# Down projection of a feed-forward block: column groups in pairs, two of eight tile pairs with seven block products

## What is computed

```python
hn = rms_norm(h, norm_ffn[i])
h = h + jnp.square(jax.nn.relu(hn @ ffn_w1[i])) @ ffn_w2[i]      # 256x2048 @ 2048x8192, then 256x8192 @ 8192x2048
gate = jax.nn.sigmoid(rms_norm(h, norm_ple[i]) @ ple_w_gate[i])
h = h + (p[i] @ ple_w_proj[i]) * gate
```

## Time and profile before

| | |
|---|---|
| median of 3 runs | 2211.09 us |
| span of the profiled execution | 2209.0 us |
| PE busy | 2197.2 us (99%) |
| DVE busy | 1445.2 us (65%) |
| ACT busy | 1106.9 us (50%) |
| POOL busy | 550.7 us (25%) |
| mean granted TensorE clock | 0.999 |

### The profile page before, as it was taken

One profiled execution on the slowest core, in us unless ns is written; L12 is line 12 of the kernel. 1 busy time (PEld: TensorE's weight loads), 2 busy tenths in 40 slices (PEclk: granted clock), 3 DMA queues, 4 the chain that ended last, 5 costly groups with the idle time before them and its releaser, 6 DMA issues.

```text
span 2209.0 us, 34195 instructions
## 1 busy us (share of the span) xinstructions
PE 2197.2 (99%) x11625; PEld 1878.9 (85%) x11625; DVE 1445.2 (65%) x1925; ACT 1106.9 (50%) x1654; POOL 550.7 (25%) x531
## 2 busy tenths in 40 slices
PE   9999999999999999999999999999999999999998
PEld 7888988888888888888888887888888888888887
DVE  6877765555664565555566667567785688756875
ACT  6445555453453454445455455565553455534553
POOL 3202220350240141053000033005540245403431
PEclk9999999999999999999999999999999999999999
DMA  7675335556555555556555653545555555555554
GB/s 254 232 230 163 115 128 204 170 190 208 191 190 192 189 189 192 186 192 193 187 185 179 227 171 135 193 160 188 195 188 196 192 183 192 189 195 192 186 209 149
DMA packets 118072, 414.21 MB, mean 188 GB/s; under 512 B 12896, under 2 KB 18048, under 8 KB 117472
## 3 DMA queue, kind: packets, MB, share of 16 engines
q1 hardware_dynamic: 111600, 401.37, 53.9%
q10 hardware_dynamic: 6384, 11.70, 1.7%
HBM read 409.29 MB, written 2.15 MB: 186 GB/s over the span
## 4 chain that ended last, share of the span: by engine, by line
PE 98%; DVE 1%; ACT 1%; issue 0%; DMA 0%; DVEq 0%; ACTq 0%
PE bank L486 33%; PE bank L494 17%; PE bank L543 7%; PE bank L545 7%; PE bank L544 7%; PE bank L1059 4%; PE bank L1060 4%; PE bank L1061 4%; PE bank L599 1%; PE bank L601 1%; PE bank L600 1%; PE bank L619 1%; PE bank L994 1%; PE bank L656 1%; PE bank L796 1%; PE bank L798 1%
## 5 line engine op out<-in xcount | busy, mean ns | idle before, releaser
L1100 DVE TENSOR_TENSOR wboth<-raw,wboth 128x1024 fp32r<-128x1024 f32 x756 | 982.2, 1302 | 607.8 <-ACT wboth L1802 607.1
L1802 ACT CAST wboth<-raw 128x1024 fp32r<-128x1024 f32 x756 | 790.9, 1049 | 711.5 <-PE bank L545 241.6
L486 PE MATMUL bank<-A,wboth 128*128 128x512 f32 x2928 | 705.1, 391 | 0.3 <-DVE wboth L1100 0.3
L486 PEld LDWEIGHTS bank<-A,wboth 128*128 128x128 f32 x2928 | 537.0, 188 | 104.6 <-issue 1.0
L494 PEld LDWEIGHTS bank<-A,wboth 128*128 128x128 f32 x2928 | 376.7, 191 | 14.8
L494 PE MATMUL bank<-A,wboth 128*128 128x256 f32 x2928 | 384.0, 283 | 0.0
L543 PE MATMUL bank<-wboth,H 128*128 128x512 f32 x576 | 224.6, 390 | 0.0
L545 PE MATMUL bank<-wboth,H 128*128 128x512 f32 x576 | 224.2, 389 | 0.0
L544 PE MATMUL bank<-wboth,H 128*128 128x512 f32 x576 | 224.1, 389 | 0.0
L2257 POOL TENSOR_TENSOR bias<-z,rs 128x256 f32<-128x256 f32 x64 | 75.7, 1182 | 481.2 <-DVE z L1131 391.6
L2257 POOL TENSOR_TENSOR PT<-z,rs 128x256 f32<-128x256 f32 x88 | 73.4, 835 | 465.4 <-DVE z L1131 464.8
(11 more groups left out here) (293 smaller groups left out, 2409.1 us busy)
## 6 DMA issues: line engine op xcount, KB each, us to landing
raw<-wstream SPq DMA_DIRECT2D x756, 512.0 KB, 3.3
bias<-bias_rows ACTq DMA_DIRECT2D x6, 512.0 KB, 5.4
x<-xrows ACTq DMA_DIRECT2D x1, 2048.0 KB, 10.0
bias<-grows ACTq DMA_DIRECT2D x2, 1024.0 KB, 6.1
out<-x SPq DMA_DIRECT2D x8, 256.0 KB, 2.1
x<-xT SPq DMA_DIRECT2D x7, 256.0 KB, 4.6
pA<-bias_rows ACTq DMA_DIRECT2D x2, 512.0 KB, 8.9
Sm<-grows ACTq DMA_DIRECT2D x1, 1024.0 KB, 5.8
```

The lines of the kernel that those rows point to most:

```text
L486: last = nc.tensor.matmul(bank(j)[:, :], whi[:, s, cols(i)], moving(j, k), start=(k == 0), stop=(k == K - 1))
L1100: V.tensor_tensor(wlo[:, s, :], raw[:, s, :], whi[:, s, :].bitcast(F32), ALU.subtract).then_inc(lo_ready, 1)
L1802: C.copy(whi[:, s, :], raw[:, s, :]).then_inc(hi_ready, 1)
```

## The change

In fd0, fd1 and fd2 two groups of 512 columns are taken together: a piece now holds one row of tiles (128 hidden values) by 1024 columns, and a column pair (`cp` 0 and 1) has 16 pieces. It accumulates into four banks, banks 0 to 3 for the first pair (`main_bank`), 4 to 7 for the second. Two of the eight pairs of pieces (`FAST` = 3 and 5: pieces 6 and 7, 10 and 11) see their product as one of 2 x 2 blocks (two halves of the tokens, two tiles of hidden values, two halves of the columns) and form it with seven block products of sums of blocks in place of eight. Four more banks (`side_bank`) hold the products that go into more than one block.

The sums are made so: POOL makes those of `H` in the up stage (`mix`, three operations behind the 8th and the 12th unit); ACT and POOL split them. DVE (`t_first`) and POOL (`t_rest`) make those of the weights, ACT (`t_highs`) and DVE (`t_lows`) split them. In the end DVE adds the side banks to `x` and to two scratch tiles (`sides_in`), POOL adds the scratch tiles (`corners`), and DVE adds the main banks (`mains_in`). The counters are old semaphores used again (`Again`). PE waits for four banks at the start of a column pair, and the projection's third group waits for `mains_in` of fd2. The loops over the two halves of a down stage are unrolled on PE, DVE and ACT, and POOL's loop over the units is unrolled too. fd3 stays as it was. The stream of the weights is laid out to suit, on the host.

```diff
+FAST = (3, 5)
+FAST_LAST = 13
+CARRY_IN = 16 + 1
...
-                    with pe.Fori(0, 2) as it:
-                        for f in range(2):
-                            down(it, f)
+                    for cp in range(2):
+                        down_pair(c, cp)
+
+            def product(bank, a_hi, a_lo, w_hi, w_lo, start=False, stop=False):
+
+                nc.tensor.matmul(bank[:, :], a_hi, w_hi, start=start, stop=False)
+                nc.tensor.matmul(bank[:, :], a_hi, w_lo, start=False, stop=False)
+                return nc.tensor.matmul(bank[:, :], a_lo, w_hi, start=False, stop=stop)
+
+            def down_pair(c, cp):
+
+                _, fd, o = chunk_at(c)
+                p = o * 64 + (PB[fd] + 16 * cp)
+                for j in range(4):
+                    pe.wait_ge(z_ready, o * 24 + (UB[fd] + (8 if cp else j + 1)))
+                for i in range(16):
...
+                    pe.wait_ge(lo_ready, p + (i + 1))
+                    if cp == 0:
+                        pe.wait_ge(ff_ready, c * CH + (i + 1))
...
+                    if not second:
...
+                        product(side_bank(cp, ONE), H[:, i, 0, 0:P], H[:, i, 1, 0:P], whi[:, s, half[0]], wlo[:, s, half[0]],
+                                lone, final).then_inc(piece_used, 1)
+                        continue
+                    product(main_bank(cp, 0), H[:, i, 0, 0:P], H[:, i, 1, 0:P], whi[:, s, half[0]], wlo[:, s, half[0]])
+                    product(main_bank(cp, 2), mixed[0][:, n, 3, :], mixed[1][:, n, 3, :], whi[:, s, half[1]], wlo[:, s, half[1]]).then_inc(piece_used, 1)
+                    t0 = c * 8 + (4 * cp + 2 * n)
+                    pe.wait_ge(*t_lo.at(t0 + 1))
+                    product(side_bank(cp, FIVE), mixed[0][:, n, 1, :], mixed[1][:, n, 1, :], Tcopy[0][:, 0, :], Tcopy[1][:, 0, :], lone, final)
+                    product(side_bank(cp, SEVEN), mixed[0][:, n, 0, :], mixed[1][:, n, 0, :], Tcopy[0][:, 1, :], Tcopy[1][:, 1, :], lone, final)
+                    pe.wait_ge(*t_lo.at(t0 + 2))
+                    product(side_bank(cp, SIX), mixed[0][:, n, 2, :], mixed[1][:, n, 2, :], Tcopy[0][:, 2, :], Tcopy[1][:, 2, :], lone, final)
+                    product(main_bank(cp, 1), H[:, i, 0, P:2 * P], H[:, i, 1, P:2 * P], Tcopy[0][:, 3, :], Tcopy[1][:, 3, :]).then_inc(t_used.sem, 1)
...
+                if f == 2:
+                    pe.wait_ge(*banks_taken.at(8 * (FF_CHUNKS - 1)))
...
+            def t_first(c, o, p0, q, n):
...
+                V.tensor_tensor(Tsum[:, 0, :], raw[:, x, 0:WIDE], raw[:, x, WIDE:], ALU.add).then_inc(t_sum.sem, 1)
+                dve.wait_ge(raw_landed[y], o * 256 + ((p0 + q + 1) // SLOTS + 1) * 16)
+                V.tensor_tensor(Tsum[:, 1, :], raw[:, x, WIDE:], raw[:, y, WIDE:], ALU.add).then_inc(t_sum.sem, 1)
+
+            def t_lows(c, i, n):
...
+                for h in range(2):
+                    dve.wait_ge(*t_hi.at(t0 + (h + 1)))
+                    V.tensor_tensor(Tcopy[1][:, 2 * h:2 * h + 2, :], Tsum[:, 2 * h:2 * h + 2, :], Tcopy[0][:, 2 * h:2 * h + 2, :].bitcast(F32),
+                                    ALU.subtract).then_inc(t_lo.sem, 1)
...
+            def sides_in(c, o, fd, cp):
+
+                dve.wait_ge(*t_used.at(c * 4 + (2 * cp + 2)))
...
+                V.tensor_copy(cross, one).then_inc(side_copied.sem, 1)
+                dve.wait_ge(*side_copied.at(c * 2 + (cp + 1)))
+                V.tensor_tensor(corner, six, cross, ALU.subtract).then_inc(z_ready, 1)
+                V.tensor_tensor(quarter(cp, 0, 0), quarter(cp, 0, 0), one, ALU.add).then_inc(z_ready, 1)
+                dve.wait_ge(z_ready, z0 + 1)
+                V.tensor_tensor(cross, corner, five, ALU.subtract).then_inc(z_ready, 1)
+                V.tensor_tensor(quarter(cp, 1, 0), quarter(cp, 1, 0), seven, ALU.add)
+                V.tensor_tensor(quarter(cp, 1, 1), quarter(cp, 1, 1), seven, ALU.subtract).then_inc(z_ready, 1)
+
+            def mains_in(c, o, fd, cp):
+
+                dve.wait_ge(piece_used, o * 64 + (PB[fd] + SLOTS + 16 * cp + 16))
+                dve.wait_ge(z_ready, o * 24 + (4 + UB[fd] + 4 * cp + 4))
+                dve.wait_ge(*corners_added.at(c * 6 + (3 * cp + 3)))
+                for j in range(4):
+                    dst = quarter(cp, j % 2, j // 2)
+                    V.tensor_tensor(dst, dst, main_bank(cp, j)[:, :], ALU.add).then_inc(banks_taken.sem, 1)
+
+            def down_pairs(c, fd, o):
+
+                p, p0 = o * 64 + PB[fd], PB[fd]
+                for q in range(LEAD, 32 + AHEAD):
...
+                    if before is not None and y:
+                        t_lows(c, q - 1, before)
+                    if second:
+                        dve.wait_ge(*t_more.at(c * 8 + (q // 16 * 4 + 2 * n + 2)))
+                    if AHEAD <= q:
+                        split_lo(p + q, (p0 + q) % SLOTS, WIDE if second == 0 else PW)
+                    if after is not None and not x:
+                        t_first(c, o, p0, q + 1, after)
+                    cp, i = divmod(q - LEAD, 16)
+                    if cp < 2 and i == FAST_LAST:
+                        sides_in(c, o, fd, cp)
+                    if (cp, i) in ((1, CARRY_IN - 16), (2, CARRY_IN - 16)):
+                        mains_in(c, o, fd, cp - 1)
...
+            def t_highs(c, i, n):
...
+                C.copy(Tcopy[0][:, 0:2, :], Tsum[:, 0:2, :]).then_inc(t_hi.sem, 1)
+                act.wait_ge(*t_more.at(s0 * 2 + 2))
+                C.copy(Tcopy[0][:, 2:4, :], Tsum[:, 2:4, :]).then_inc(t_hi.sem, 1)
...
+            def mix(c, n, a, b):
...
+                G.tensor_tensor(mixsum[:, n, 0:2, :], both, a[:, late].unsqueeze(1).to_broadcast([P, 2, P]), ALU.subtract).then_inc(mix_sum.sem, 1)
+                pool.wait_ge(*mix_sum.at(s0 + 1))
+                G.tensor_tensor(mixsum[:, n, 2, :], mixsum[:, n, 1, :], a[:, early], ALU.add).then_inc(mix_sum.sem, 1)
+                pool.wait_ge(*mix_sum.at(s0 + 2))
+                G.tensor_tensor(mixsum[:, n, 3, :], b[:, early], mixsum[:, n, 2, :], ALU.subtract).then_inc(mix_sum.sem, 1)
+
+            def t_rest(c, cp, i, n):
...
+                G.tensor_tensor(Tsum[:, 2, :], Tsum[:, 0, :], raw[:, y, WIDE:], ALU.add).then_inc(t_more.sem, 1)
+                pool.wait_ge(*t_more.at(t0 + 1))
+                G.tensor_tensor(Tsum[:, 3, :], Tsum[:, 2, :], raw[:, y, 0:WIDE], ALU.add).then_inc(t_more.sem, 1)
+
+            def corners(c, o, fd, cp):
+
+                pool.wait_ge(z_ready, o * 24 + (4 + UB[fd] + 4 * cp + 4))
+                for t, f, src, op in ((1, 0, corner, ALU.subtract), (0, 1, cross, ALU.add), (1, 1, cross, ALU.add)):
+                    dst = xN[:, t, (2 * cp + f) * WIDE:(2 * cp + f + 1) * WIDE]
+                    G.tensor_tensor(dst, dst, src, op).then_inc(corners_added.sem, 1)
...
-                with pool.Fori(0, 4) as it:
+                for it in range(4):
...
+                    if fast and 2 * it + 1 in FAST:
+                        mix(c, FAST.index(2 * it + 1), tB[:, 2, :], tB[:, 3, :])
+                if fast:
+                    down_pairs(c, fd, o)
```

More of the change, by code:

```diff
@@ L174, in cmp_due, with fast_piece @@
     return [g for g in range(KVG) if (8 * g + CMP_AT[step] if g < KVG - 1 else CMP_AT_LAST[step]) == i]
+FAST = (3, 5)
+FAST_LAST = 13
+CARRY_IN = 16 + 1
+def fast_piece(i):
+    m, second = divmod(i % 16, 2)
+    return (FAST.index(m), second) if m in FAST else (None, None)
 def turn_of(n):
@@ L191, in __call__, with __init__, at @@
         self.eng.wait_ge(self.sem, self.n)
+class Again:
+    def __init__(self, sem, reached):
+        self.sem, self.reached = sem, reached
+    def at(self, n):
+        return self.sem, n + self.reached
 def program(nc, xT, pT, wstream, consts, setup, params, grows, xrows, out):
@@ L220, in program @@
         pA = sb("pA", [P, 2, 2, S], FR)
+        with nc.sbuf_tensor("Tboth", [P, 2, 4, WIDE], FR) as Tboth:
+            pass
         y = sb("y", [P, DT, S])
@@ L250, in ring @@
             return flat[:, a:a + n * w].rearrange("p (n w) -> p n w", n=n)
+        Tsum = ptf.rearrange("p (n c) -> p n c", n=4)
+        Tcopy = [Tboth[:, h, :, :] for h in range(2)]
+        kTf = kT[:, :, :, :].rearrange("p a g c -> p (a g c)")
+        corner, cross = kTf[:, 0:WIDE], kTf[:, WIDE:2 * WIDE]
+        mixf = [vT[:, 2 * h:2 * h + 2, :].rearrange("p a c -> p (a c)") for h in range(2)]
+        mixed = [m.rearrange("p (n i q) -> p n i q", n=len(FAST), i=4) for m in mixf]
         zr, sq = ring(bflat, 0), ring(bflat, 4 * S, 8)
@@ L355, in program, with main_bank, side_bank @@
         dn_half = sem("dn_half")
+        def main_bank(cp, j):
+            return psum[4 + j] if cp else psum[(UB["fd0"] + j) % 4]
+        def side_bank(cp, j):
+            return psum[(UB["fd0"] + j) % 4] if cp else psum[4 + j]
+        SIX, ONE, FIVE, SEVEN = range(4)
         NORM_AT = {"kv": 3, "ff0": 4, "k2": 0, "up0": 6}
@@ new lines, in mains_in @@
+            def mains_in(c, o, fd, cp):
```

(40 more changed lines are left out.)

61 lines of the change are left out of this document (49 added, 12 removed).

## The result

The changed kernel takes **2228.4 us**, the median of 4 runs (2227.77 to 2231.04); the kernel before took 2211.24 us on the same chip (4 runs, 2210.38 to 2211.74). The ratio is 1.008, with a 95% interval of 1.0068 to 1.0092: slower by 0.8%, where 2230.8 us was forecast.

The account below looks back on a forecast made before the run. PE, 99% busy and fed without gaps, was taken as the only bound. Terms −8.2 + 7.9 + 2 x 6.1 + 3.3 + 4.5 = +19.7 on 2209.0 us of span, plus 2.1, gave 2230.8 us; range 2214 to 2242.

Parts of the forecast that it names:

- the clock stays: Rival: the clock stays up or comes back at once after PE's pauses, same sum without 4.5, 2226.3 us; chance 0.20.
- no lateness is kept: Rival: ff1 and ff2 stay in the quiet rhythm and mix fits POOL's pause, +2.6, 2213.7 us; chance 0.11.
- the last evacuation is not waited for: Rival: all three down-stage starts cost nothing, −5.9, 2205.2 us, faster than before; chance 0.04.
- Fast pairs starve: Rival: POOL's additions meet DVE's, the margin goes and 1 us is lost at each of 12 pairs, 2243 us; chance 0.12.
- Removed matmuls: In fd0 to fd2, seven products for eight remove 36 matmuls of 0.227 us each: −8.2 us.
- The start of fd0: PE waits 5.9 us for ff0's last evacuation, plus 2.0 for two mixes: 7.9 us.
- The starts of fd1 and fd2: Each starts 6.1 us late: 1.3 quiet-rhythm wait, 2.8 lateness from work behind the down stage before, 2.0 for mixes.
- The rule of turn-taking: Behind fd0 and fd1, POOL's corner additions alternate with DVE's subtractions, making the first evacuation 3.9 us late; 2.8 was taken.
- The projection: Its third group waits for fd2's mains_in, 2.3 to 4.4 us; 3.3 taken.
- The clock: After PE's pauses at three places the clock falls, about 3 us at half speed each: 1.5 each, 4.5 us in all.
- Inside the down stages: The new sums, casts and subtractions are hidden by the timetable; no cost, no PE wait over 0.5 us in fast pairs.
- The margin of 2.7 us: At the second fast pair, DVE's split weight sums end at 4.8 and 6.0 us; PE needs them at 7.5 and 8.8.

Follow-up runs that it names:

- e1_wait: Kernel before, with PE waiting for all four main banks instead of two at the starts of fd0 to fd2, down groups written out: 2221.98 us.
- e3_defer: Changed kernel, with the fourth bank's products of pieces 0 to 2 made behind piece 2's others, so three banks suffice to start: 2213.14 us.
- e2_dummy: Changed kernel, with 16 unneeded matmuls put into PE's wait for the fourth bank at each of the three turns: 2221.33 us.
- e8_eight: Changed kernel, with all eight block products of a fast pair made instead of seven, sums, casts and waits kept: 2236.96 us.
- e4_mixless: Changed kernel, with POOL's mix additions cut from 128 columns to 1, casts and semaphores kept: 2223.99 us.
- e9_mains: Changed kernel, with the corner additions on DVE and the four main-bank additions moved three subtractions ahead: 2223.53 us.
- e7_defer_dve: Changed kernel, with the fourth bank's first products put off, and corner additions and two last weight sums of each fast pair on DVE: 2208.49 us.

## Why the prediction was right, and where it was not

The forecast was 2230.8 us, in the range of 2214 to 2242, and the time is 2228.4. The mechanism is that of the text: PE waits at the turn to each down stage for the last evacuation, and e1_wait and e3_defer show it from both sides. Of the rivals, "the clock stays" is out by e2_dummy, "no lateness is kept" by the 4.4 us at fd1 and fd2 against 1.24 in e1_wait, and "the last evacuation is not waited for" by the 14.7 us. "Fast pairs starve" is out for the changed kernel, which waits at none. Term by term:

- **Removed matmuls**, −8.2: held. e8_eight gives 8.6 us for 36. The 131 ns of the Trainium skill ("TensorE: Matmul & The Clock Gate", "Back-to-back issue gap") would give an estimate of 4.7; the measurement decides for 227.
- **The start of fd0**, 7.9 forecast, 6.0 measured. The wait alone was put at 5.9 from the earlier trace rows and is 5.54 in e1_wait: I had counted from a weight load, which PE does ahead. Two mixes were put at 2.0 and cost 1.4 (e4_mixless). Together that is 0.9 too much, and the loop of ff0 explains it: from its first evacuation to its sixteenth it takes 80.34 us in e1_wait and 79.18 in e4_mixless, which has the new loop without the mixes' work. Of these 1.16 us, 0.76 are gained in the first four steps; the other eleven are 5.52 us each in place of 5.56 on average (the 5.58 of the earlier trace rows is one long step). PE gave 0.26 back between the evacuation's end and its first matmul. The 0.04 can be seen: DVE's subtraction ahead of an evacuation takes 1.28 us in e1_wait, where POOL's last operation runs into it (to 481.57, DVE from 481.37), and 1.23 in the changed kernel, where it doesn't (to 481.66, DVE from 481.68). I had costed the unrolling at nothing; that the unrolling of POOL's loop is the cause was not tried.
- **The starts of fd1 and fd2**, 6.1 each, 4.43 and 4.31 measured. The quiet part is 1.24 (1.3 forecast) and the mixes 1.4 to 1.5 (2.0). The lateness at the start of ff1 was put at 2.8: the first evacuation came 584.04 − 575.78 = 8.26 us after PE's turn in place of 5.95, 2.3 late. The sum 1.24 + 1.45 + 2.3 is 5.0, of which the shorter step takes some 0.6 off. Of the 2.8, 1.8 was put down to `mains_in` and 1.0 to the corners; the corners moved to DVE brought 0.6 and `mains_in` moved ahead another 0.7. The rest, 0.9, stays in e9_mains and is DVE's own work, which the timetable had only as single items behind a cast.
- **The rule of turn-taking** (the Trainium skill, "SBUF — State Buffer", "Who interferes with whom") held for the operations: three corners took 6.67 us beside subtractions, 2.2 each, against the 1.7 of the earlier trace rows, and the three subtractions 5.68 in place of 3.49. It did not give the 3.9 us of lateness that I drew from it. The fourth subtraction had to wait for a cast in any case, so only what it took itself counts, 1.84 in place of 1.23.
- **The projection**, 3.3 forecast, 2.7 measured.
- **The clock**, 4.5 forecast, 7.5 measured. The fall came 2.7 to 3.4 us after PE stopped, near the 2 to 3 of the earlier trace rows. The way back was the term that was mis-sized: half speed during work lasted 4.3 to 5.7 us, not 3.
- **Inside the down stages**, nothing forecast and nothing measured, but the cover was named wrongly. The margin of 2.7 us before a fast pair was worked out for the second pair. For the first one e3_defer shows −1.3: POOL's subtraction of the mixed blocks doubles a subtraction of DVE just before, and DVE then waits for POOL's last sum. e7_defer_dve takes away the second alone, and PE no longer waits. What hid it in the changed kernel was, by the traces, the idle time at the turn.

The sum of the terms was +19.7 and the span grew by 17.0. The waits were forecast 23.4 and came to 17.5 (14.7 + 2.7, unrounded), 6 too many; the clock was 3 too little. The total is nearer than its terms because these two have opposite signs, and that is luck.

## What to carry to other kernels

Where one engine is the bound and has no gap, look at what it waits for at each turn of stages before counting what is saved inside them. Waiting for four free banks where two were enough cost 10.8 us here (e1_wait), more than the seven-for-eight products saved (8.2), and making the products of the last bank later gave 15.3 of the changed kernel's time back. A loop over engines whose step nearly equals the bound's step (5.53 against 5.56 us here) makes next to nothing good: a few tenths at its first unit are paid at its last. Moving work within a full queue wins only the pauses in it (0.65 us of 2.5 here). And idle time of one stage can be the cover of another: mend one wait, then read the trace again for what it had hidden.
